# Two of a pair's twelve weight low parts on GpSimd instead of VectorE in a hybrid RWKV-7 and pooling layer

## The reference, cut to what matters

```
h = RMSNorm_pre(x)
z = h @ w_in                      # 2048 -> [r | k | v | g | u_pool | g_pool | gate_a | gate_b]
r, k, v = token shift of z's first 3*1024 columns
S_t = S_{t-1} diag(w_t) + (S_{t-1} a_t) b_t^T + v_t k_t^T ;  o_t = S_t r_t    # 16 heads of 64
y_a = (GroupNorm(o) + bonus) * silu(g)
y_b = pooled branch * silu(g_pool)
m = sigmoid(gate_a) * (y_a @ w_branch[0]) + sigmoid(gate_b) * (y_b @ w_branch[1])
x = x + RMSNorm_post(m @ w_out)
x = x + sigmoid(x @ w_ple_gate) * (p @ w_ple)
```

## Time and profile before

| | us |
|---|---|
| median of 3 runs | 1145.81 (1145.09 to 1146.93) |
| profiled execution | 1146.05 |
| its span | 1144.5 |
| TensorE busy | 1117.6 |
| VectorE busy | 794.6 |
| ScalarE busy | 543.7 |
| GpSimd busy | 159.7 |

### The profile page before, as it was taken

One profiled execution on the slowest core, in us unless ns is written; L12 is line 12 of the kernel. 1 busy time (PEld: TensorE's weight loads), 2 busy tenths in 40 slices (PEclk: granted clock), 3 DMA queues, 4 the chain that ended last, 5 costly groups with the idle time before them and its releaser, 6 DMA issues.

```text
span 1144.5 us, 23678 instructions
## 1 busy us (share of the span) xinstructions
PE 1117.6 (98%) x8594; PEld 1072.2 (94%) x8594; DVE 794.6 (69%) x1681; ACT 543.7 (48%) x960; POOL 159.7 (14%) x273
## 2 busy tenths in 40 slices
PE   5999999999999999999999999999999999999998
PEld 5889998999999999999999999999999999989998
DVE  5979897979798888988678544444444497685442
ACT  5444747566574747474643333333333343354342
POOL 2422131314131221221140000000000500000000
PEclk9999999999999999999999999999999999999999
DMA  9714433434343343443464555555555965516551
GB/s 239 199 38 124 122 104 111 113 110 115 110 128 97 107 127 99 115 121 103 129 184 130 152 147 154 153 144 149 147 148 147 283 186 148 149 54 167 168 161 38
DMA packets 279708, 155.10 MB, mean 136 GB/s; under 512 B 7717, under 2 KB 275661, under 8 KB 279012
## 3 DMA queue, kind: packets, MB, share of 16 engines
q1 hardware_dynamic: 272528, 139.65, 43.6%
q0 software_dynamic: 6992, 14.87, 4.9%
q10 hardware_dynamic: 148, 0.04, 0.0%
HBM read 149.15 MB, written 5.61 MB: 135 GB/s over the span
## 4 chain that ended last, share of the span: by engine, by line
PE 70%; DVE 17%; issue 6%; DMA 4%; ACT 3%; DVEq 0%; SPq 0%; ACTq 0%; POOL 0%; POOLq 0%
PE acc L1753 14%; PE acc L1755 13%; PE acc L1754 13%; PE wide L1755 6%; PE wide L1754 6%; PE wide L1753 6%; PE wide L1777 4%; DVE wl L1116 3%; PE wide L1860 2%; PE wide L2157 2%; DVE rn L1221 1%; PE wide L1772 1%; DMA wraw<-in_w_out 1%; ACT wh L719 1%; DVE kkn L1511 1%
## 5 line engine op out<-in xcount | busy, mean ns | idle before, releaser
L1116 DVE TENSOR_TENSOR wl<-wraw,wh 128x1024 fp32r<-128x1024 f32 x256 | 315.8, 1240 | 168.6 <-ACT wh L719 166.5
L719 ACT CAST wh<-wraw 128x1024 fp32r<-128x1024 f32 x256 | 266.8, 1048 | 213.3 <-PE acc L1755 124.0
L1753 PE MATMUL acc<-hh,wh 128*128 128x320 f32 (+1 forms) x1084 | 349.4, 322 | 8.6 <-DVE rS L1132 5.6
L1754 PE MATMUL acc<-hl,wh 128*128 128x320 f32 (+1 forms) x1084 | 336.5, 310 | 0.0
L1755 PE MATMUL acc<-hh,wl 128*128 128x320 f32 (+1 forms) x1084 | 335.8, 310 | 0.0
L1753 PEld LDWEIGHTS acc<-hh,wh 128*128 128x128 f32 x1084 | 204.2, 188 | 13.1 <-issue 7.4
L1754 PEld LDWEIGHTS acc<-hl,wh 128*128 128x128 f32 x1084 | 204.1, 188 | 0.3
L1755 PEld LDWEIGHTS acc<-hh,wl 128*128 128x128 f32 x1084 | 204.1, 188 | 0.0
L1753 PE MATMUL acc<-x1h,wh 128*128 128x320 f32 x256 | 81.0, 316 | 0.0
L1753 PE MATMUL acc<-mh,wh 128*128 128x320 f32 x256 | 79.4, 310 | 0.2 <-DVE wl L1116 0.2
L1755 PE MATMUL acc<-x1h,wl 128*128 128x320 f32 x256 | 79.1, 309 | 0.0
(11 more groups left out here) (424 smaller groups left out, 2003.7 us busy)
## 6 DMA issues: line engine op xcount, KB each, us to landing
wraw<-in_w_in SPq DMA_DIRECT2D x160, 512.0 KB, 3.8
wraw<-in_w_branch SPq DMA_DIRECT2D x32, 512.0 KB, 4.0
wraw<-in_w_out SPq DMA_DIRECT2D x32, 512.0 KB, 4.3
wraw<-in_w_ple_gate SPq DMA_DIRECT2D x32, 512.0 KB, 4.2
xt<-in_x_prompt SPq DMA_DIRECT2D x2, 1024.0 KB, 7.2
S0n<-in_state_wkv POOLq DMA_DIRECT2D x64, 32.0 KB, 3.6
out<-so POOLq DMA_DIRECT2D x16, 128.0 KB, 4.1
xt<-in_x_prompt POOLq DMA_DIRECT2D x2, 1024.0 KB, 7.8
```

What stands on the lines that cost most here:

```text
L719: A.copy(wh[:, slot, :], wraw[:, slot, :]).then_inc(s["hi_ready"], 1)
L1116: V.tensor_tensor(wl[:, slot, :], wraw[:, slot, :], wh[:, slot, :].bitcast(F32), ALU.subtract).then_inc(s["lo_ready"], 1)
L1753: M.matmul(out[:, 0:width], wh[:, slot, wcol], hi, start=first, stop=False)
L1754: M.matmul(out[:, 0:width], wh[:, slot, wcol], lo, start=False, stop=False)
```

## The change

In each of the eight mixes the low parts of chunk 7 (step 4) and chunk 13 (step 10) are subtracted by GpSimd. `split_low` waits until all low parts before its chunk are written, and for the chunk's high part, and then does the same subtraction and counts up `lo_ready`. It is called at the head of `mix_out`, in front of the wait for `tails`, and again behind `lora_low`, in front of the store of `eo`. VectorE drops `go(4)` and `go(10)`. Ahead of `go(5)` and `go(11)` it now waits until GpSimd's low part is counted, so that `lo_ready` keeps the order of the chunks.

```diff
+            def split_low(r, j):
+                at_chunk = (r + 1) * CH_STEP + BASE_STEP + j + AHEAD
+                slot = (j + AHEAD) % SLOTS
+                wait_alone("lo_ready", at_chunk)
+                wait_alone("hi_ready", at_chunk + 1)
+                gp_.tensor_tensor(wl[:, slot, :], wraw[:, slot, :], wh[:, slot, :].bitcast(F32), ALU.subtract
+                                  ).then_inc(s["lo_ready"], 1)
+
             def mix_out(r, q=None):
+                split_low(r, 4)
                 wait_alone("tails_ready", r * 8 + 4)
...
                 if q is not None:
                     lora_low(q)
+                split_low(r, 10)
 
                 wait_alone("end_ready", r + 1)
...
+                def go_after_gpsimd(j):
+                    dve.wait_ge(s["lo_ready"], q * CH_STEP + (BASE_STEP + j + AHEAD))
+                    go(j)
...
-                go(4)
                 out(2)
...
-                go(5)
+                go_after_gpsimd(5)
...
-                go(10)
                 dve.wait_ge(s["dsq_ready"], r * 2 + 2)
...
-                go(11)
+                go_after_gpsimd(11)
```

## The result

The changed kernel takes 1177.11 us (1173.92 to 1180.23, 4 runs) against 1145.45 us before (1144.85 to 1146.93, 4 runs): 2.7% slower, ratio 1.0274, 95% interval 1.0242 to 1.0307. The direction and both places were forecast; the size, 31.7 us against 21.4, lies outside the range.

The account below looks back on a forecast made before the run. TensorE, 98% busy, was taken as the bound, with VectorE pacing one half of each mix; 6.2 us at chunk 13 plus 15.2 at chunk 7 added 21.4 to 1145.8, giving 1167.2 us, range 1162.8 to 1170.4.

Parts of the forecast that it names:

- Both halves of a mix: From `O_l` to `rS` VectorE sets the pace; from `rS` to the outputs `O` TensorE does, covering VectorE's changes.
- the worth of the removed instructions: Two `wl` per mix off VectorE: chunk 7's worth 0, chunk 13's at most 0.28 us per mix.
- Place A, the race: Chunk 7: GpSimd starts 0.02 to 0.06 us before VectorE's `parts`, delaying it and `rS` 1.92 us per mix, 15.2 us.
- Place B: Chunk 13: GpSimd's subtraction blocks VectorE's `dsq_l`, which starts in effect 0.77 us later per mix, 6.2 us in all.
- D: Time of one GpSimd 128x1024 subtraction, taken as 2.1 us, range 1.83 to 2.3, from 128x512 and 96x128 rows.
- Stores, loads and the two waits of `go_after_gpsimd`: Later `eo` stores come back to the same place, moved loads still precede TensorE's use, and both waits pass at once.

Follow-up runs that it names:

- e8: The kernel before, with GpSimd subtracting chunk 7 when the change does and VectorE subtracting it again at its old place: 1173.63 us, ratio 1.0245.
- e3: The change, with each GpSimd subtraction waiting for one more signal, behind `rS` for chunk 7 and `dsq_l` for chunk 13: 1148.91 us, 1.0033 of the kernel before.
- e7: Only chunk 7 moved to GpSimd, with one more wait, for a signal long given, before its subtraction: 1147.78 us, 1.0025 of the kernel before.
- e2: The kernel before with only chunk 13 (step 10) moved to GpSimd, chunk 7 staying on VectorE: 1152.68 us, ratio 1.0062.
- e5: The change, with 20 unused transposes put into TensorE's queue ahead of the wait for `rS` in each mix: 1169.37 us, 1.0214 of the kernel before.
- e1: The kernel before with only chunk 7 (step 4) moved to GpSimd, chunk 13 staying on VectorE: 1173.06 us, ratio 1.0238.

## Why the prediction was wrong

- **Both halves of a mix, and the worth of the removed instructions:** right. Nothing at A (e8), 0.28 us at B at most; e3 shows `dsq_l` starting as soon as `dsq_h` is there.
- **Place A, the race:** right, and in all eight mixes, but narrowly. The lead was 0.06 to 0.08 us in seven mixes and 0.14 in the eighth, in place of 0.02 to 0.06, and one queue step, reckoned at 0.2 us and worth 0.1 in e7, reverses it in those seven. Its formula, D - 0.2 per mix, gives 2.17 with the measured D; `parts` grew by 2.12.
- **Place B:** right in mechanism; D - 1.33 gives 1.04, TensorE waits 1.1 us, alone 7.8 us (e2).
- **D, the first step that failed:** 2.37 us, above the 2.3 at which the range of D ended. The 128x512 row is of an operation with repeated operands, and 10% on top of its double was too little; the slope that gave 1.83 us joined it to a 96x128 row with plain operands, which is another kind. The estimate by the Trainium skill's figure ("GPSIMD Engine Reference", "Performance versus the Vector engine"), 2.25 us, was nearer than 2.1 and still low. With D = 2.37 the forecast's sum is 8 x (2.17 + 1.04) = 25.7 us, 4.3 more than forecast, and the time 1171.5 us.
- **The clock, the step that was missing:** the sum took TensorE's work for constant while its wait went from 0.76 to 2.9 us. Behind five of these eight waits the granted clock stood at 1.2 GHz for a stretch. e5 takes the idleness away and gets some 7 us back with both blocks in place. 25.7 and some 6 make up the 31.7, so the clock is the larger of the two misses.
- Stores, loads and the two waits of `go_after_gpsimd` cost nothing that shows in the change, as forecast: its periods with the full clock are 3.2 us longer, which the two blocks explain (2.12 + 1.04). e3 shows when such a wait does cost.

## What to carry to other kernels

Before work moves to GpSimd, write down for the whole length of its new instruction what VectorE executes beside it: a two-operand SBUF operation that comes second waits to the end, however small it is, and here an 80-element one cost 2.1 us; operations with one SBUF operand are the place to put it. Move what stands in the half of the loop that VectorE paces, and start it from a signal behind the operation that must not wait, not from the earliest one. And where a forecast adds a wait of TensorE of some microseconds, ask what its clock does behind it. The list of waits is not the price of a stop: here 0.76 us listed were 1.03 us of TensorE's time.

## What the runs showed of the hardware that was not expected

- GpSimd's fp32 subtraction of 128x1024 takes 2.37 us with two plain operands, 2.26 times the 1.05 us of a 128x512 product with repeated ones.
- A few hundredths of a microsecond decide which engine goes first: 0.02 us were enough for VectorE, 0.05 for GpSimd (both in e7).
- TensorE's granted clock fell behind idle stretches of 2.9 us in all eight mixes of e1 and of e8 and in five of the change's, but neither behind the one of e7 nor behind the one of e3, and never behind those of 1.1 us. What singles out those in which it didn't fall stays open; since e1 differs from the change by the second place alone, it isn't more idleness in a mix.
